# Layer 1's modulation units: sixteen for latent tokens alone, all 28 at other slabs

## Chip, cores and metric

The kernel runs on one core of a Trainium2 chip. The metric is the device time of one execution in microseconds (us), the median of several runs. The core's engines work side by side, each through its own list of instructions in order, and wait for each other by semaphores: TensorE (PE, matmuls; its weight loads are shown as PEld), VectorE (DVE), ScalarE (ACT), GpSimd (POOL) and SyncE (SP), which here issues all the transfers from memory.

## The reference, cut to what matters

A trunk of two layers. Each has a token mixer (gated linear attention in layer 0, windowed attention in layer 1) and a SwiGLU network (FFN). It works on 512 latent tokens (`x`) and 256 context tokens (`ctx`), with 1024 features. Shift, scale and gate of each sublayer come from two vectors, one for the latent tokens and one for the context tokens:

```
mod_x = einsum('bd,lde->lbe', silu(c), w_ada) + b_ada      # w_ada: 2 layers x 1024 x 6144
mod_c = einsum('d,lde->le', silu(c_ctx), w_ada) + b_ada
for i in range(DEPTH):                                     # DEPTH = 2
    last = i == DEPTH - 1
    sh1, sc1, g1, sh2, sc2, g2 = split(mod_x[i], 6)        # 1024 values each
    csh1, csc1, cg1, csh2, csc2, cg2 = split(mod_c[i], 6)
    hx = rmsnorm(x, norm_mix[i]) * (1 + sc1) + sh1
    hc = rmsnorm(ctx, norm_mix[i]) * (1 + csc1) + csh1
    ox, oc = mixer(hx, hc)                                 # context also feeds the latent tokens
    x = x + g1 * ox
    x = x + g2 * swiglu(rmsnorm(x, norm_ffn[i]) * (1 + sc2) + sh2)
    if not last:
        ctx = ctx + cg1 * oc
        ctx = ctx + cg2 * swiglu(rmsnorm(ctx, norm_ffn[i]) * (1 + csc2) + csh2)
return rmsnorm(x, norm_final)
```

In layer 1 the context tokens need only `csh1` and `csc1`: its gates and the FFN's modulation are used for latent tokens alone.

## The kernel before

Everything that is multiplied is split in two: a high part (rounded, made by ScalarE) and a low part (the rest, made by VectorE), and each product is three matmuls. Weights come in slabs of 256 columns, numbered `n` in the order of TensorE. For each slab SyncE loads the raw weights (`load_slab`), ScalarE makes the high part (`split`, or `form_high`), VectorE the low part (`split`, line 2005, or `form_low`, line 2562), and TensorE multiplies. Two sets of buffers alternate, so that `load_slab(n)` waits until slab n - 2 is done.

The stretch in question is the FFN of layer 0, slabs `F0` = 16 to `KV0` - 1 = 61. It has six parts. A part has input slabs (4, 4, 4, 3, 3, 4 of them: one row of 128 hidden units each, gate and up) and then four output slabs (`OUT0`), each for 256 of the 1024 output features and over the part's 4 or 3 rows. Part 0 begins at F0, part 1 at F0 + 8, part 2 at F0 + 16, part 3 at F0 + 24, part 4 at F0 + 31, part 5 at F0 + 38. From F0 + 3 on, input slabs are computed as seven products of half size (`SEVEN`), with sums of weight blocks (`form_sum`, line 2557) and of results (`part_sum` on ScalarE, line 1752; `gate_sum_one`, `up_sum_one` at lines 2577 and 2583, and so on, on VectorE). Seven-product slabs are 84 matmuls over 384 columns; output slabs of four rows are 48 over 512 or 256 columns.

The modulation vectors are made in units of 256 columns of `w_ada`. Units 12 to 15 are of layer 0, units 16 to 39 of layer 1. Unit a of layer 1 covers the columns (128 each) 16 + 2a and 17 + 2a of `mods`; from unit 24 on these are columns 64 to 95: gate of the mixer, and shift, scale and gate of the FFN. `UNIT_AT` says at which slab each of the units 12 to 39 is made. Before, that is: at the last input slab of part 0, the last two of parts 1 to 4 and the last three of part 5; at all four output slabs of parts 0 to 2, and at the first and third of parts 3 and 4.

A unit has these steps. SyncE loads it (1 MB, line 502) into the one buffer `ada_w`, right after the load of its slab in SyncE's queue, once the unit before it is accumulated (`ada_done`); the next slab's load is queued behind. VectorE adds up 8 blocks x 2 kinds of token, sixteen operations over 128x256 elements (`unit_acc`, lines 2106 and 2110), each of which waits for the one before the last. At the next slab TensorE sums over partitions by four small matmuls (`unit_sum`), after the first block of an output slab or the second product of a seven-product slab. Then VectorE closes the unit (`store_sum`, lines 2088, 2092, 2095) by three small operations.

The order on VectorE is written out by hand. In an output slab it is: `store_sum` of the slab before, `unit_acc`, `split(n + 1)`, `residual` (line 2121, once TensorE is done with the slab), so TensorE's next slab waits for the accumulations. In a seven-product slab with another behind it, `unit_acc` stands after `up_sum_one(n)` and ahead of the last four `form_low` of the next slab and of `times_gate` (line 2598), for which ScalarE's `high7(n)` waits; ScalarE's `part_sum(n + 1, 0)` is queued behind `high7(n)`, and TensorE's fourth product of slab n + 1 waits for it.

Of the kernel before, what the change touches and what calls it, by code (L numbers as in the profile page):

```python
# [30 lines left out]
AX = mybir.AxisListType  # L31

P = 128
D = 1024
DC = D // P
# [21 lines left out]
for part_, (f_, fc_) in enumerate(PARTS0):  # L57
    n_ = F0 + f_ + 4 * part_
    for j_ in range(fc_):
        IN0[n_ + j_] = f_ + j_  # L60
        if f_ + j_ >= 3:
            SEVEN[n_ + j_] = f_ + j_ - 3
        if part_ == 0 and j_ == 3 or 0 < part_ < 5 and j_ >= fc_ - 2 or part_ == 5 and j_ > 0:
            UNIT_AT[n_ + j_] = 12 + len(UNIT_AT)
    for e_ in range(4):
        OUT0[n_ + fc_ + e_] = (part_, e_, fc_)
        if part_ < 3 or part_ < 5 and e_ % 2 == 0:
            UNIT_AT[n_ + fc_ + e_] = 12 + len(UNIT_AT)
# [15 lines left out]
def trunk(nc, x, c, ctx_in, c_ctx, w_ada, b_ada, norm_mix, norm_ffn, gla_w_in, gla_w_gate_up, gla_b_gate_up,  # L84
# [240 lines left out]

        return n if n < R0 else n - R_SLOTS

    U1 = F0 - R_SLOTS

    def sum_no(a):  # L330

        return a if a < V0 else a - U1 + V0

    def u_set(a):

        return int(a >= U1)

# [337 lines left out]
    def _(pe):  # L675
# [439 lines left out]
        def ffn(l, n0, segs, per):  # L1115
            n, done = n0, l * FC
            for part, (f0, fc) in enumerate(PARTS):
                lead, after = int(part == 0), int(part == 2)
                if lead:

                    first_slab(n, 2 * l, segs, turn=U1 - 1 if l == 0 else None)
                    slab(n + 1, 0, h_in, segs, k_wait=h_wait(2 * l + 1, per), joint=True)
                m = n + 2 * lead
                with pe.Fori(0, fc // 2 - lead - after) as i:
                    for e in range(2):
                        slab(m + e, i, h_in, segs)
                if after:

                    for e in range(2):
                        m = n + fc - 2 + e  # L1130
                        slab(m, 0, h_in, segs)
                n += fc
                done += fc

                def ready(k, done=done, fc=fc):

                    if k in (0, fc - 1):
                        pe.wait_ge(a_ok, done - (k == 0))
                with pe.Fori(0, 2 - int(l == 1 and after)) as i:
                    for e in range(2):  # L1140
                        slab(n + e, i, a_in, segs, kc=fc, k_wait=ready)
                if l == 1 and after:
                    slab(n + 2, 0, a_in, segs, kc=fc)
                    slab(n + 3, 0, a_in, segs, kc=fc, by_chunk=True, between=early_result)
                n += 4
# [22 lines left out]
                              stop=(k == 3 and i == 2), skip=True)  # L1168
            last.then_inc(pd_ok if j < 6 else slab_done, 1)

        first_slab(F0, 0, BOTH, turn=U1 - 1)
        slab(F0 + 1, 0, h_in, BOTH, k_wait=h_wait(1, 2), joint=True)
        slab(F0 + 2, 0, h_in, BOTH)
        for n in range(F0 + 3, KV0):
            if n in SEVEN:
                for j in range(7):
                    product(n, j)
                    if j == 1 and n - 1 in UNIT_AT:
                        unit_sum(UNIT_AT[n - 1])
            else:  # L1180
                part, e, fc = OUT0[n]
                done = PARTS0[part][0] + fc

                def ready(k, done=done, fc=fc):

                    if k in (0, fc - 1):
                        pe.wait_ge(a_ok, done - (k == 0))
                slab(n, 0, a4_in, BOTH, kc=fc, k_wait=ready,
                     before={(0, 1): lambda: unit_sum(UNIT_AT[n - 1])} if n - 1 in UNIT_AT else {})


        first_slab(KV0, KV_EDGE, BOTH)
# [174 lines left out]
    def _(act):  # L1367
# [386 lines left out]
        def gate_one(n):  # L1754
            act.wait_ge(g_ok, SEVEN[n] + 1)
            silu(tmp[n % 2][:, 0:HT])
# [32 lines left out]
        form_high(F0 + 3, 2)  # L1789
        up0(F0 + 2, 2)  # L1790
        for n in range(F0 + 3, KV0):
            if n in SEVEN:
                after = n + 1 in SEVEN
                head = n - 1 not in SEVEN
# [14 lines left out]
                part_sum(n, 1)  # L1809
                if after:  # L1810
                    form_high(n + 1, 1)
                gate_one(n)
                if after:
                    form_high(n + 1, 2)
# [13 lines left out]
            else:  # L1828
                part, e, fc = OUT0[n]
                if e < 3:  # L1830
                    split(n + 1, 0, fc)
                elif part < 5:
                    for j in range(3):
                        form_high(n + 1, j)
                else:
                    split(n + 1)
                if part == 5:
                    for ch in range(2):
                        squares("ffn0", 2 * e + ch, 0)
                    for ch in range(2):  # L1840
                        raw_high("ffn0", KV_EDGE, 2 * e + ch, BOTH)
# [158 lines left out]
    def _(dve):  # L2000
# [82 lines left out]
        def store_sum(a, i=0):  # L2083

            dve.wait_ge(turned, a + 2 + i)
            dve.wait_ge(or_ok, u_set(a) + 1)
            part = u_acc[u_set(a)][:, 0, 0:P].rearrange("p (c n) -> p c n", n=32)
            dve.tensor_tensor(part, bank(7, 0, P).rearrange("p (c n) -> p c n", n=32),
                              every[u_set(a)][:, :].rearrange("p (o n) -> p o n", o=1).to_broadcast([P, 4, 32]), ALU.mult)\
               .then_inc(up_ok, 1)  # L2090
            dve.wait_ge(up_ok, 2 * sum_no(a) + 1 + i * 2)
            dve.tensor_reduce(den[:, :], part, AX.X, ALU.add).then_inc(up_ok, 1)
            dve.wait_ge(up_ok, 2 * sum_no(a) + 2 + i * 2)
            e = unit_cols(a) + i * 2
            dve.tensor_tensor(mods[:, bass.ds(e, 2), :], den[:, :].rearrange("p (m e) -> p e m", m=2),
                              v3(vec[:, bass.ds(V_BADA + e, 2)], 2), ALU.add).then_inc(mod_ok, 1)

        def unit_acc(a, i=0):

            dve.wait_ge(in_unit, 16 * (a + 1) + i * 16)  # L2100
            acc = u_acc[u_set(a)]
            for k in range(DC):
                for m in range(2):
                    j = 2 * k + m
                    if k == 0:
                        last = dve.tensor_scalar(acc[:, m, :], ada_w[:, 0, :], c_pre[:, 0, m:m + 1], None, ALU.mult)  # L2106
                    else:

                        dve.wait_ge(ua_ok, 15 * sum_no(a) + j - 1 + i * 15)
                        last = dve.scalar_tensor_tensor(acc[:, m, :], ada_w[:, k, :], c_pre[:, k, m:m + 1],  # L2110
                                                        acc[:, m, :], ALU.mult, ALU.add)
                    last.then_inc(ua_ok if j < 15 else ada_done, 1)
# [19 lines left out]

        dve.wait_ge(const_ok, N_CONST)
        dve.memset(c_pre[:, :, :], 0.0).then_inc(c_zero, 1)
        dve.memset(resets[:, :], 1.0).then_inc(resets_ok, 1)
        dve.wait_ge(resets_ok, 1)
        dve.memset(resets[:, 0:T:P], 0.0)
# [288 lines left out]
        for n in range(GO0, F0):  # L2426
            split(n + 1)
            plain(n, "gla", 2 * (n - GO0), 16, BOTH, False)
            raw_low(0, 2 * (n - GO0), BOTH)
            store_unit(unit_of(n))  # L2430
            if n == F0 - 1:
                dve.wait_ge(mod_ok, U1 + 1)
                shifts(0, 24)
            raw_low(0, 2 * (n - GO0) + 1, BOTH)

# [204 lines left out]
        form_sum(F0 + 3, 2)  # L2640
        form_low(F0 + 3, 1)
        form_low(F0 + 3, 2)
        up0(F0 + 2, 2)
        for n in range(F0 + 3, KV0):
            a_ = UNIT_AT.get(n)
            last_a = UNIT_AT.get(n - 1)
            if n in SEVEN:
                after = n + 1 in SEVEN
                if n - 1 not in SEVEN:
# [11 lines left out]
                    form_sum(n + 1, 0)  # L2661
                    form_low(n + 1, 0)
                gate_sum_one(n)
                if last_a is not None:
                    store_sum(last_a)
                if after:
                    form_sum(n + 1, 1)
                    form_sum(n + 1, 2)
                    form_low(n + 1, 1)
                    form_low(n + 1, 2)  # L2670
                    up_sum_one(n)
                    if a_ is not None:
                        unit_acc(a_)
                    form_low(n + 1, 3)
                    form_sum(n + 1, 3)
                    up_sum_two(n)
                    form_low(n + 1, 4)
                    form_low(n + 1, 5)
                else:
                    if a_ is not None:  # L2680
                        unit_acc(a_)
                    up_sum_one(n)
                    split(n + 1, 0, OUT0[n + 1][2])
                    up_sum_two(n)
                gate_sum_two(n)
                if after:
                    form_low(n + 1, 6)
# [1 line left out]
                low0(n)  # L2689
            else:  # L2690
                part, e, fc = OUT0[n]
                if last_a is not None:
                    store_sum(last_a)
                if part == 5 and e == 0:
                    scale_rows(48 + 8, V_NMIX + 8)
                if a_ is not None:
                    unit_acc(a_)
                if e < 3:
                    split(n + 1, 0, fc)
                elif part < 5:  # L2700
# [4 lines left out]
                    form_low(n + 1, 1)  # L2705
                else:
                    split(n + 1)
                if part < 5:
                    residual(n, 0, BOTH, 40, 2 * e, None)
                    if e == 3:  # L2710
# [228 lines left out]
```

## Time and profile before

| | us |
|---|---|
| median of 3 runs | 1681.86 (1681.06 to 1684.31) |
| the profiled execution, its own time | 1687.11 |
| its span, first to last instruction | 1685.4 |
| TensorE busy | 1584.0 |
| VectorE busy | 1083.0 |
| ScalarE busy | 665.2 |

The profile is of one execution. Its page gives the busy time of each engine, and the views cut it further: by stretch, by who waited for whom, or instruction by instruction. A busy TensorE may still be slow, since its clock is granted by the chip at full (1.0) or at half rate.

### The profile page before, as it was taken

To read this page: it belongs to the slowest core of one execution; us is meant where nothing else is said; L and a number is where in the kernel's file an instruction comes from. 1 tells how busy PE (TensorE), PEld (TensorE's weight loads), DVE (VectorE), ACT (ScalarE), POOL (GpSimd) and SP (SyncE) were. 2 spreads that over 40 slices of the span, in tenths; PEclk is the share of its full clock that TensorE was granted. 3 is DMA by queue.
4 is the path that set the end of the run, shared out by engine and by line. 5 is a ranking of instruction groups with operands and counts; after the bars stand their busy time and mean duration, and the time that the engine had idled before them with its cause. 6 is when DMAs were issued, how large, how long until landed. Compare 5 with 4: busy or idle time off the path is not lost.

```text
span 1685.4 us, 23337 instructions
## 1 busy us (share of the span) xinstructions
PE 1584.0 (94%) x9196; PEld 1363.8 (81%) x9196; DVE 1083.0 (64%) x1907; ACT 665.2 (39%) x1051; POOL 100.1 (6%) x95
## 2 busy tenths in 40 slices
PE   7999999999988989989898899999999999999998
PEld 4789988888886977978788788877778788888886
DVE  5655456444698888888878787788874633333334
ACT  5325367433641421423323234557763522222223
POOL 0000000000000000000000000006650000000002
PEclk8999999999999999989989899999999999999999
DMA  9333200033124324234233422431002332333322
GB/s 337 98 125 101 75 26 26 26 100 101 51 70 155 101 78 147 85 124 142 79 110 94 119 75 88 125 89 37 1 1 75 88 90 97 100 100 100 100 88 88
DMA packets 197842, 156.47 MB, mean 93 GB/s; under 512 B 7138, under 2 KB 194702, under 8 KB 197742
## 3 DMA queue, kind: packets, MB, share of 16 engines
q1 hardware_dynamic: 197742, 155.10, 30.2%
q8 instruction: 67, 1.10, 0.3%
q14 instruction: 33, 0.27, 0.1%
HBM read 149.84 MB, written 2.10 MB: 90 GB/s over the span
## 4 chain that ended last, share of the span: by engine, by line
PE 68%; DVE 18%; ACT 6%; DMA 4%; issue 3%; SPq 1%; DVEq 0%; ACTq 0%
PE ps L677 66%; DVE u_acc L2110 7%; DMA ada_w<-in_w_ada 2%; DVE w_lo L2005 1%; PE ps L1257 1%; DVE t_lo L2562 1%; DMA w_raw<-in_ffn_w_in 1%; ACT w_hi L1375 1%; ACT pr L1959 1%; DVE t_sum L2557 1%; DVE u_acc L2106 1%; DMA ada_pre<-in_w_ada 1%; DVE w_lo L2562 1%; DVE scaled L2061 1%; DVE tmp L2598 1%
## 5 line engine op out<-in xcount | busy, mean ns | idle before, releaser
L677 PE MATMUL ps<-h_hi,w_lo 128*128 128x512 f32 (+2 forms) x936 | 338.0, 361 | 0.0
L677 PE MATMUL ps<-h_hi,w_hi 128*128 128x512 f32 (+1 forms) x784 | 293.7, 375 | 4.2 <-DVE w_lo L2005 4.0
L677 PE MATMUL ps<-h_lo,w_hi 128*128 128x512 f32 (+1 forms) x784 | 286.4, 365 | 0.0
L2005 DVE TENSOR_TENSOR w_lo<-w_raw,w_hi 128x2048 fp32r<-128x2048 f32 (+1 forms) x57 | 128.5, 2254 | 198.4 <-ACT w_hi L1375 198.4
L677 PEld LDWEIGHTS ps<-h_hi,w_lo 128*128 128x128 f32 x936 | 177.4, 190 | 24.4
L677 PE MATMUL ps<-a_hi,w_lo 128*128 128x512 f32 (+1 forms) x528 | 192.4, 364 | 0.0
L1375 ACT ACTIVATE w_hi<-w_raw 128x2048 fp32r<-128x2048 f32 (+1 forms) x57 | 107.3, 1883 | 195.1 <-DMA w_raw<-in_ffn_w_in 98.3
L2110 DVE SCALAR_TENSOR_TENSOR u_acc<-ada_w,c_pre,u_acc 128x256 f32<-128x256 f32 x448 | 180.1, 479 | 0.0
L677 PEld LDWEIGHTS ps<-h_hi,w_hi 128*128 128x128 f32 x784 | 148.5, 189 | 34.5 <-issue 6.2
L677 PEld LDWEIGHTS ps<-h_lo,w_hi 128*128 128x128 f32 x784 | 148.7, 190 | 24.0
L677 PE MATMUL ps<-a_hi,out_hi_w 128*128 128x512 f32 (+1 forms) x352 | 128.6, 365 | 35.2 <-DVE w_lo L2005 33.7
L665 POOL TENSOR_SCALAR pr<-pr,rden 128x384 f32<-128x384 f32 x64 | 82.5, 1296 | 887.0 <-DVE rden L2845 886.7
L677 PE MATMUL ps<-a_lo,out_hi_w 128*128 128x512 f32 (+1 forms) x352 | 124.4, 353 | 0.0
L2121 DVE SCALAR_TENSOR_TENSOR xT<-ps,mods,xT 128x512 f32<-128x512 f32 (+2 forms) x142 | 82.5, 639 | 55.7 <-PE ps L677 55.7
L677 PEld LDWEIGHTS ps<-a_hi,w_lo 128*128 128x128 f32 x528 | 103.2, 195 | 15.6
L677 PEld LDWEIGHTS ps<-a_hi,out_hi_w 128*128 128x128 f32 x352 | 70.0, 199 | 51.1 <-DVE w_lo L2005 36.5
L677 PE MATMUL ps<-h_hi,form_hi 128*128 128x384 f32 x304 | 103.7, 341 | 5.0 <-DVE w_lo L2562 4.6
L677 PE MATMUL ps<-h_sums_lo,form_hi 128*128 128x384 f32 x304 | 106.7, 351 | 0.0
L677 PE MATMUL ps<-h_lo,form_hi 128*128 128x384 f32 x304 | 104.4, 343 | 0.0
L677 PEld LDWEIGHTS ps<-a_lo,out_hi_w 128*128 128x128 f32 x352 | 70.2, 200 | 7.1
L677 PE MATMUL ps<-h_sums_hi,form_hi 128*128 128x384 f32 x152 | 55.1, 363 | 21.3 <-ACT tmp L1752 21.3
L1732 ACT ACTIVATE form_hi<-t_sum 128x512 fp32r<-128x512 f32 x76 | 47.0, 627 | 70.3 <-DVE t_sum L2557 62.6
(320 smaller groups left out, 3125.1 us busy)
## 6 DMA issues: line engine op xcount, KB each, us to landing
w_raw<-in_ffn_w_in SPq DMA_DIRECT2D x88, 512.0 KB, 5.1
ada_w<-in_w_ada SPq DMA_DIRECT2D x41, 1024.0 KB, 5.3
w_raw<-in_gla_w_in SPq DMA_DIRECT2D x24, 512.0 KB, 4.9
w_raw<-in_ffn_w_out SPq DMA_DIRECT2D x40, 256.0 KB, 5.3
w_raw<-in_ffn_w_out SPq DMA_DIRECT2D x16, 512.0 KB, 4.4
ada_pre<-in_w_ada SPq DMA_DIRECT2D x7, 1024.0 KB, 11.5
w_raw<-in_gla_w_o SPq DMA_DIRECT2D x8, 512.0 KB, 6.8
w_raw<-in_swa_w_o SPq DMA_DIRECT2D x8, 512.0 KB, 4.6
```

The lines of the kernel that those rows point to most:

```text
L665: pool.tensor_scalar(pr[i % 4][:, 0:384], pr[i % 4][:, 0:384], rden[:, i % 4:i % 4 + 1], None, ALU.mult)\
L677: return pe.matmul(o, w, r, start=start, stop=stop, skip_group_check=skip)
L1257: last = pe.transpose(bank(4 + r, t * P, P), pr[i % 4][:, t * P:(t + 1) * P], ident[:, :])
L1375: act.activation(hi_of(n)[:, 0:kc, :], raw_of(n)[:, 0:kc, :], ACT.Copy).then_inc(whi_ok, 1)
L1732: act.activation(form_hi[j][:, :, :], form_from(n, j, w_raw, t_sum), ACT.Copy).then_inc(fh_ok, 1)
L1959: act.activation(pr[i % 4][:, 0:nk + 1], ps[:, sb:sb + nk + 1], ACT.Exp, bias=neg_max[:, i % 4:i % 4 + 1], scale=HD ** -0.5, accum_out=den ...
L2005: dve.tensor_tensor(w_lo[s][:, 0:kc, :], raw_of(n)[:, 0:kc, :], hi_of(n)[:, 0:kc, :].bitcast(F32), ALU.subtract).then_inc(wlo_ok, 1)
L2061: dve.scalar_tensor_tensor(scaled_t[ch % 2][:, s[0]:s[1]], xT[:, ch, s[0]:s[1]], amul[:, ch, c_:c_ + 1], rb[:, s[0]:s[1]], ALU.mult, ALU.m ...
L2106: last = dve.tensor_scalar(acc[:, m, :], ada_w[:, 0, :], c_pre[:, 0, m:m + 1], None, ALU.mult)
L2110: last = dve.scalar_tensor_tensor(acc[:, m, :], ada_w[:, k, :], c_pre[:, k, m:m + 1], acc[:, m, :], ALU.mult, ALU.add)
L2121: last = dve.scalar_tensor_tensor(xs, seg(slab_banks(n), ch, sg), mods[:, bass.ds(gate + d0 + ch, 1), int(sg == CTX)], xs, ALU.mult, ALU.add)
L2562: dve.tensor_tensor(form_from(n, j, w_lo, t_lo), form_from(n, j, w_raw, t_sum), form_hi[j][:, :, :].bitcast(F32), ALU.subtract).then_inc(f ...
```

## The change

1. `UNIT_AT` has other slabs: the last two input slabs of part 0, all four of part 1, the last two of parts 2 to 4, none of part 5. The output slabs stay as they are. Unit 12 is thus at slab F0 + 2, which isn't a seven-product slab, and its `unit_acc` stands by itself ahead of `up0(F0 + 2, 2)`. Before, units 12 to 39 were at 12 input slabs and 16 output slabs, and they are after.
2. Units from `LATENT` = 24 on are made for latent tokens alone: eight accumulations in place of sixteen, the even blocks in one half of `u_acc` and the odd in the other; the closing sum runs over both halves. The column sum on TensorE stays as it is. Columns 64 to 95 of `mods` for context tokens are set to zero once at the start.
3. TensorE, ScalarE and VectorE get branches for units below `U1` to be made on TensorE (`0 < now < U1`). With `U1` = 12 and units from 12 on, no slab takes them.

```
-        if part_ == 0 and j_ == 3 or 0 < part_ < 5 and j_ >= fc_ - 2 or part_ == 5 and j_ > 0:
+        if part_ == 0 and j_ >= 2 or part_ == 1 or 1 < part_ < 5 and j_ >= fc_ - 2:
             UNIT_AT[n_ + j_] = 12 + len(UNIT_AT)
...
-    U1 = F0 - R_SLOTS
+    U1 = 12
+    LATENT = 24
...
+    def acc_base(a):
+
+        whole = V0 + LATENT - U1
+        return 15 * min(sum_no(a), whole) + 7 * max(sum_no(a) - whole, 0)
...
@@ store_sum
+            if a >= LATENT:
+
+                both = u_acc[1][:, 0, 0:P].rearrange("p (m e n) -> p e m n", m=2, e=2)
+                dve.tensor_reduce(den[:, 0:2], both, AX.XY, ALU.add).then_inc(up_ok, 1)
+                dve.wait_ge(up_ok, 2 * sum_no(a) + 2)
+                dve.tensor_tensor(mods[:, e:e + 2, 0], den[:, 0:2], vec[:, V_BADA + e:V_BADA + e + 2], ALU.add)\
+                   .then_inc(mod_ok, 1)
+                return
...
@@ unit_acc
+            if a >= LATENT:
+
+                for k in range(DC):
+                    half = acc[:, k % 2, :]
+                    if k < 2:
+                        last = dve.tensor_scalar(half, ada_w[:, k, :], c_pre[:, k, 0:1], None, ALU.mult)
+                    else:
+
+                        dve.wait_ge(ua_ok, acc_base(a) + k - 1)
+                        last = dve.scalar_tensor_tensor(half, ada_w[:, k, :], c_pre[:, k, 0:1], half, ALU.mult, ALU.add)
+                    last.then_inc(ua_ok if k < DC - 1 else ada_done, 1)
+                return
...
         dve.memset(c_pre[:, :, :], 0.0).then_inc(c_zero, 1)
+        dve.memset(mods[:, 64:96, 1], 0.0)
...
         form_low(F0 + 3, 2)
+        unit_acc(12)
         up0(F0 + 2, 2)
```

## Rows read from the trace of the kernel before

**Rows 1.** The page: busy us (share of the span) xinstructions, by engine.
```profile
PE 1584.0 (94%) x9196; PEld 1363.8 (81%) x9196; DVE 1083.0 (64%) x1907; ACT 665.2 (39%) x1051; POOL 100.1 (6%) x95
```

**Rows 2.** TensorE's waits, 504 to 1030 us: us in total, times, longest.
```profile
PE ps L677 <- DVE w_lo L2005: 33.7, 13, 3.9
PE ps L677 <- ACT tmp L1752: 21.3, 6, 3.7
```

**Rows 3.** Stages: stretch, length, busy by engine, granted clock, DMA share, GB/s.
```profile
642.71:665.75 23.04, 19.91 (x112) 15.87 (x113) 20.44 (x50) 2.41 (x4) 0.00 (x0) 0.93 0.53 160
665.75:731.84 66.09, 62.56 (x352) 60.94 (x353) 55.67 (x106) 28.55 (x53) 0.00 (x0) 0.95 0.32 97
731.84:779.06 47.22, 40.68 (x225) 32.51 (x225) 40.88 (x97) 5.90 (x8) 0.00 (x0) 0.89 0.43 134
779.06:830.54 51.48, 47.95 (x269) 46.65 (x269) 44.54 (x89) 20.94 (x39) 0.00 (x0) 0.93 0.34 102
830.54:869.88 39.34, 31.79 (x170) 24.98 (x169) 28.85 (x64) 5.68 (x8) 0.00 (x0) 0.87 0.31 94
869.88:919.55 49.67, 46.15 (x262) 45.38 (x261) 42.41 (x83) 20.47 (x38) 0.00 (x0) 0.97 0.33 98
919.55:958.69 39.14, 31.58 (x169) 24.87 (x169) 28.84 (x64) 5.69 (x8) 0.00 (x0) 0.87 0.34 105
958.69:1029.06 70.37, 63.16 (x355) 61.63 (x353) 60.08 (x119) 28.53 (x52) 0.00 (x0) 0.95 0.33 98
```

**Rows 4.** VectorE's timeline, part 0's output: start us, us, instruction, [idle <-releaser].
```profile
508.99 0.28 DVE L2088 TENSOR_TENSOR u_acc<-ps,every 128x128 f32<-128x128 f32 x1
...
509.71 0.61 DVE L2106 TENSOR_SCALAR u_acc<-ada_w,c_pre 128x256 f32<-128x256 f32 x2
510.24 5.62 DVE L2110 SCALAR_TENSOR_TENSOR u_acc<-ada_w,c_pre,u_acc 128x256 f32<-128x256 f32 x14
...
521.18 0.62 DVE L2106 TENSOR_SCALAR u_acc<-ada_w,c_pre 128x256 f32<-128x256 f32 x2 [0.57 <-DMA ada_w<-in_w_ada]
```

**Rows 5.** SyncE's timeline in the same slab.
```profile
515.89 0.37 SPq L502 DMA_DIRECT2D ada_w<-in_w_ada  x1
```

**Rows 6.** VectorE's timeline, ends of two output slabs of part 5.
```profile
1046.52 2.19 DVE L2121 SCALAR_TENSOR_TENSOR xT<-ps,mods,xT 128x256 f32<-128x256 f32 x4 [0.81 <-PE ps L677]
...
1054.86 1.54 DVE L2121 SCALAR_TENSOR_TENSOR xT<-ps,mods,xT 128x256 f32<-128x256 f32 x3 [0.66 <-PE ps L677]
```

**Rows 7.** Instructions on the accumulator: ns min/median/max, first and last start.
```profile
L677 PE MATMUL ps<-u_acc,ones x256: 272/297/423, 77.2 to 1030.7; 128*32 128x128 f32 x128
```

**Rows 8.** VectorE's timeline, input slabs of parts 0 and 1.
```profile
488.36 1.01 DVE L2530 TENSOR_TENSOR tmp<-tmp,ps 128x256 f32<-128x256 f32 x2
...
565.14 0.55 DVE L2583 TENSOR_TENSOR tmp<-ps,tmp 128x384 f32<-128x384 f32 x1
...
573.11 0.96 DVE L2538 TENSOR_TENSOR a_lo<-tmp,a_hi 128x768 fp32r<-128x768 f32 x1 [0.91 <-ACT a_hi L1764]
...
587.67 0.96 DVE L2538 TENSOR_TENSOR a_lo<-tmp,a_hi 128x768 fp32r<-128x768 f32 x1 [0.91 <-ACT a_hi L1764]
...
594.73 0.61 DVE L2106 TENSOR_SCALAR u_acc<-ada_w,c_pre 128x256 f32<-128x256 f32 x2
```

**Rows 9.** TensorE's timeline: five instructions ahead of which it stood still.
```profile
608.21 0.69 PE L677 MATMUL ps<-h_sums_hi,form_hi 128*128 128x384 f32 x1 [3.52 <-ACT tmp L1752]
...
720.95 0.69 PE L677 MATMUL ps<-h_sums_hi,form_hi 128*128 128x384 f32 x1 [3.52 <-ACT tmp L1752]
...
842.42 0.80 PE L677 MATMUL ps<-a_hi,out_hi_w 128*128 128x512 f32 x1 [3.85 <-DVE w_lo L2005]
...
998.33 0.44 PE L677 MATMUL ps<-h_sums_hi,form_hi 128*128 128x384 f32 x1 [3.52 <-ACT tmp L1752]
...
1019.02 0.44 PE L677 MATMUL ps<-h_sums_hi,form_hi 128*128 128x384 f32 x1 [3.69 <-ACT tmp L1752]
```

**Rows 10.** VectorE's timeline at the start.
```profile
6.52 0.85 DVE L2141 COPY xT<-ps 128x256 f32<-128x256 f32 x2 [0.26 <-PE ps L820]
```

More of the change, by code:

```diff
@@ L1119, in ffn @@
                 if lead:
-                    first_slab(n, 2 * l, segs, turn=U1 - 1 if l == 0 else None)
+                    first_slab(n, 2 * l, segs)
                     slab(n + 1, 0, h_in, segs, k_wait=h_wait(2 * l + 1, per), joint=True)
@@ L1169, in product @@
             last.then_inc(pd_ok if j < 6 else slab_done, 1)
-        first_slab(F0, 0, BOTH, turn=U1 - 1)
+        first_slab(F0, 0, BOTH, turn=11)
         slab(F0 + 1, 0, h_in, BOTH, k_wait=h_wait(1, 2), joint=True)
@@ L1174, in _ @@
         for n in range(F0 + 3, KV0):
+            now, old = UNIT_AT.get(n, 0), UNIT_AT.get(n - 1, 0)
             if n in SEVEN:
@@ L1177, in _ @@
                     product(n, j)
-                    if j == 1 and n - 1 in UNIT_AT:
-                        unit_sum(UNIT_AT[n - 1])
+                    if j == 1 and old >= U1:
+                        unit_sum(old)
+                    if j == 1 and 0 < now < U1:
+                        unit(now)
+                    if j == 4 and 0 < now < U1:
+                        unit_turn(now)
             else:
@@ L1187, in ready @@
                         pe.wait_ge(a_ok, done - (k == 0))
-                slab(n, 0, a4_in, BOTH, kc=fc, k_wait=ready,
-                     before={(0, 1): lambda: unit_sum(UNIT_AT[n - 1])} if n - 1 in UNIT_AT else {})
+                at_ = {}
+                if old >= U1:
+                    at_[0, 1] = lambda: unit_sum(old)
+                if 0 < now < U1:
+                    at_[0, 2] = lambda: unit(now)
+                    at_[1, fc - 1] = lambda: unit_turn(now)
+                slab(n, 0, a4_in, BOTH, kc=fc, k_wait=ready, before=at_)
         first_slab(KV0, KV_EDGE, BOTH)
@@ L1791, in _ @@
         for n in range(F0 + 3, KV0):
+            now = UNIT_AT.get(n, 0)
             if n in SEVEN:
@@ L1811, in _ @@
                     form_high(n + 1, 1)
+                if 0 < now < U1:
+                    unit_row(now)
                 gate_one(n)
@@ L1836, in _ @@
                     split(n + 1)
+                if 0 < now < U1:
+                    unit_row(now)
                 if part == 5:
@@ L2087, in store_sum @@
             part = u_acc[u_set(a)][:, 0, 0:P].rearrange("p (c n) -> p c n", n=32)
+            e = unit_cols(a) + i * 2
             dve.tensor_tensor(part, bank(7, 0, P).rearrange("p (c n) -> p c n", n=32),
@@ L2091, in store_sum @@
             dve.wait_ge(up_ok, 2 * sum_no(a) + 1 + i * 2)
+            if a >= LATENT:
[5 more added lines that the diff above has]
+                return
             dve.tensor_reduce(den[:, :], part, AX.X, ALU.add).then_inc(up_ok, 1)
             dve.wait_ge(up_ok, 2 * sum_no(a) + 2 + i * 2)
-            e = unit_cols(a) + i * 2
             dve.tensor_tensor(mods[:, bass.ds(e, 2), :], den[:, :].rearrange("p (m e) -> p e m", m=2),
@@ L2107, in unit_acc @@
                     else:
-                        dve.wait_ge(ua_ok, 15 * sum_no(a) + j - 1 + i * 15)
+                        dve.wait_ge(ua_ok, acc_base(a) + j - 1)
                         last = dve.scalar_tensor_tensor(acc[:, m, :], ada_w[:, k, :], c_pre[:, k, m:m + 1],
@@ L2431, in _ @@
             if n == F0 - 1:
-                dve.wait_ge(mod_ok, U1 + 1)
+                dve.wait_ge(mod_ok, 13)
                 shifts(0, 24)
@@ L2642, in _ @@
         form_low(F0 + 3, 2)
+        unit_acc(12)
         up0(F0 + 2, 2)
         for n in range(F0 + 3, KV0):
-            a_ = UNIT_AT.get(n)
-            last_a = UNIT_AT.get(n - 1)
+            now, old = UNIT_AT.get(n, 0), UNIT_AT.get(n - 1, 0)
             if n in SEVEN:
@@ L2663, in _ @@
                 gate_sum_one(n)
-                if last_a is not None:
-                    store_sum(last_a)
+                if old >= U1:
+                    store_sum(old)
                 if after:
@@ L2671, in _ @@
                     up_sum_one(n)
-                    if a_ is not None:
-                        unit_acc(a_)
+                    if now >= U1:
+                        unit_acc(now)
                     form_low(n + 1, 3)
@@ L2679, in _ @@
                 else:
-                    if a_ is not None:
-                        unit_acc(a_)
+                    if now >= U1:
+                        unit_acc(now)
                     up_sum_one(n)
@@ L2684, in _ @@
                     up_sum_two(n)
+                if 0 < now < U1:
+                    store_unit(now)
                 gate_sum_two(n)
@@ L2691, in _ @@
                 part, e, fc = OUT0[n]
-                if last_a is not None:
-                    store_sum(last_a)
+                if old >= U1:
+                    store_sum(old)
                 if part == 5 and e == 0:
                     scale_rows(48 + 8, V_NMIX + 8)
-                if a_ is not None:
-                    unit_acc(a_)
+                if now >= U1:
+                    unit_acc(now)
                 if e < 3:
@@ L2707, in _ @@
                     split(n + 1)
+                if 0 < now < U1:
+                    store_unit(now)
                 if part < 5:
```

## The prediction, made before the change was run

> **What bounds the kernel now.** I read the busy line of the page first: TensorE is busy for 94% of the span and VectorE for 64% [rows 1]. So time can be had only where TensorE stands still or runs slowly. The view of waits, for TensorE alone and for the stretch in which all 28 moved units lie, names two releasers: 33.7 us in 13 waits for VectorE's low halves of output slabs (line 2005), and 21.3 us in 6 waits for ScalarE's copies in seven-product slabs (line 1752) [rows 2]. The windows by stage then show a second loss. The granted clock is at its lower level (1.2 of 2.4 GHz) for part of every stage, and length x (1 - clock) is what that costs: 1.6, 3.3, 5.2, 3.6, 5.1, 1.5, 5.1 and 3.5 us in the eight stages from 642.71 us on, 28.9 us together [rows 3].
>
> What a unit costs VectorE is in the timeline of one output slab [rows 4]. The closing chain runs from 508.99 to 509.71 us (0.7 us); the sixteen accumulations run from 509.71 to 515.86 us, about 6.1 us until the next operation can start. The fourteen long ones take 5.62 us, which is one of 0.48 us and thirteen steps of 0.396 us. SyncE issues the next unit's transfer at 515.89 us [rows 5], and its accumulations start at 521.18 us, released by that transfer [rows 4]: 5.3 us. One turn of this loop is 5.3 + 6.1 = 11.4 us. TensorE needs less: two output slabs without units in the last part end 8.34 us apart [rows 6]. The eight records of a column sum last 0.30 us each but overlap [rows 7]; I take 0.5 us for them, so 8.9 us for a slab with a unit. **The output slabs are bound by the loop of transfer and accumulation, not by TensorE.**
>
> In seven-product slabs, an undisturbed one lasts 587.67 - 573.11 = 14.56 us [rows 8]. A unit delays VectorE's last products of the slab, ScalarE queues behind them, and TensorE stops at the fourth product of the next slab: 3.52 us each in parts 1 and 2 and twice, 3.52 and 3.69, in part 5 [rows 9].
>
> **The change, stage by stage.** Times are of the profiled execution.
>
> A latent unit (24 to 39) has eight accumulations. Each waits for the one before the last, as now, so I keep the step [rows 4]: 8 x 0.396 = 3.17 us less, 2.9 us left. The closing chain keeps its three operations; I count nothing for the smaller ones (between 0 and 0.2 us each).
>
> Unit 12 moves ahead of `up0(F0 + 2, 2)`, which starts at 488.36 us [rows 8]. VectorE has work without a pause from there to the output slab, so all of it comes 6.1 us later, the fourth product of slab F0 + 3 with it, and its column sum makes TensorE wait until 494.5 us. ScalarE's copies for that slab queue behind `up0`. Unit 13 then takes the place that unit 12 had, with one closing chain more: **+6.9 us** for the first output slab. From below it is 0.7 us, if a pause hid the accumulations, from above 8.5 us if low clock is added. The transfers have room: unit 12's is issued a slab earlier, unit 13's at 494.5 us for a use at 503 us. The four output slabs of part 0 have a full unit each now and after: 0. SyncE's queue there holds each slab's load behind the same kind of unit load as now.
>
> Part 1 gets full units in all four of its seven-product slabs, where two had one. The first would start after line 2583 at 565.14 + 0.47 = 565.61 us; now one starts at 594.73 in slab F0 + 10 and the stop ends at 608.21 us [rows 8, 9], 13.48 us later. So the fourth product of slab F0 + 9 comes at 579.1 us. For slabs with full units one after the other the trace has a sample: the two stops of part 5 end 20.69 us apart [rows 9], because the chain of VectorE and the slab load queued behind the unit's load take that long. Two such periods give 620.5 us against 608.21: **+12.3 us**. At best it is the three stops, two more than now, with no clock loss, +7; at worst each period is 2 us longer, +16.
>
> Part 1's output slabs 2 and 3 have units 24 and 25, latent. Loop: 5.3 + 2.9 = 8.2 us, below TensorE's 8.9, so TensorE becomes the bound: 23.04 us [rows 3] becomes 17.9, **-5.1**.
>
> Part 2, seven products: the stop shrinks from 3.52 to 0.35 us, and the low clock of its stage goes. Of the 3.3 us some lies within the stop itself: the four products from 720.95 to 731.84 us take 10.89 us [rows 3, 9] where 4/7 of 14.56, or 8.32, is undisturbed, so 2.6 us. 3.17 + 2.6: **-5.7**. Part 2, output: 47.22 us becomes 4 x 8.9 + 0.1, **-11.5**. Part 3, seven products: 3.17 and four fifths of 3.6: **-6.0**; part 4, 3.17 and four fifths of 1.5: **-4.5**.
>
> Output slabs of parts 3 and 4 (three rows, three quarters of 8.34 = 6.26 us): the first goes from 842.42 - 830.54 = 11.88 [rows 3, 9] to 8.7 us, still VectorE-bound; then 6.8, 6.3 and 6.8 us, and 0.6 us at the next slab, whose weights now land only just in time: 29.2 us against 39.34 and 39.14 [rows 3]: **-10.1 and -9.9**.
>
> Part 5 loses its three units. 4 x 14.56 + 0.4 = 58.6 us against 70.37 [rows 3], **-11.8**, and **-0.5** for the column sum in its first output slab.
>
> The memset of 32 values lies on VectorE before line 2141, which waits for TensorE (0.26 us) [rows 10]: 0, at most 0.1 us. The kernel ends with no other difference: layer 1 waits for all units at its load of Q, and the last one is now done earlier.
>
> Sum: +6.9 + 12.3 - 5.1 - 5.7 - 11.5 - 6.0 - 4.5 - 10.1 - 9.9 - 11.8 - 0.5 = **-45.9 us**. The profiled execution took 1687.11 us (span 1685.4); the median of the runs is 1681.86, 0.3% less, which leaves the difference as it is: **1636 us**.
>
> One rule prices the accumulations otherwise. The Trainium skill (VectorE: DVE Perf Modes, "The TRN2 errata") gives such an operation 58 cycles beside one for each element, at 0.96 GHz; worked out from that page as an estimate, 0.33 us for 256 elements, or 2.6 us saved in a unit and a total some 3 us longer. The trace has the duration (0.396 us), so that is used.
>
> **Rivals.**
> *The clock stays low.* The stops shrink, but the clock falls as before. For it: no stage from part 1 on is free of it, and small stops remain. Against: it goes with the stops; the stages with most of them for their length are at 0.87, the one with a single stop in 49.67 us is at 0.97 [rows 3]. It would cost the 28.9 us of the stages: -17, 1665 us. The rule that speaks for it is in the Trainium skill (TensorE: Matmul & The Clock Gate, "HAM oscillation"): a wait that comes back in each step makes the clock drop anew in each.
> *The transfer becomes the bound.* A loop of landing plus 2.9 us stays hidden only while a unit lands within 6.0 us. If contention with the slab's load, which is now issued at another moment, made it half as long again as the 5.3 us, some 7.8 us, nine output slabs are 1.8 us longer each: +16, 1652 us. Against: the unit's load is still issued ahead of the slab's, as at 515.89 us.
> *Slower: eight accumulations take as long as sixteen.* If an accumulation had to wait for the result of its predecessor, the step would be some 0.76 us (6.1/8). Then nothing is gained in parts 1 to 4, and +6.9 + 12.3 - 12.3 leaves +6.9 us: 1689 us. The gains of parts 1 to 4, 52.8 us, hang on the 3.17 us, so the sign turns where a latent unit is shorter by less than 0.4 us. Against it: the two running sums alternate as the two token kinds do now.
>
> **How the numbers follow.** Forecast 78%, with a range of its own of 1628 to 1648 from the bounds of +6.9 and +12.3 and of the unit's landing; low clock 7%, transfer 11%, slower 4%. The range of 1628 to 1655 takes in the transfer case and leaves out the clock case, the slower one and the forecast's tails. A difference below 0.2% (3.4 us) can't be told from none: faster 95%, same 1%, slower 4%.
>
> **What would show it.** Latent units of 2.9 us; output slabs of part 2 9 us apart with no wait for line 2005; stops of under 1 us in parts 2 to 4, three of about 3.6 us in part 1, none in part 5; clock 1.0 in nearly all stages after part 1; the first output slab of part 0 some 7 us later, of part 1 some 19 us later. A loop that still takes over 10 us in part 2, or a low clock there with stops gone, would prove me wrong.

## The result: 1639.4 us, 2.5% faster

The changed kernel takes 1639.41 us (median of 4 runs, 1638.66 to 1641.18), the kernel before beside it 1682.28 us. The ratio is 0.9746, with a 95% interval of 0.9729 to 0.9762: 42.9 us less, where 45.9 were forecast. The two profiled spans are 1685.4 and 1639.5 us, 45.9 us apart; the forecast was worked out from the first, so the stages are compared in them. That they differ by 3 us more than the medians comes from which executions were profiled: 1687.11 us is 4.8 above the median before, 1641.18 us is 1.8 above the median after.

TensorE's waits in the changed kernel, 504 to 1019 us, line 2026 being the old 2005, 1768 the old 1752 (us in total, times, longest). They answer to [rows 2]:

```profile
PE ps L683 <- DVE w_lo L2026: 17.9, 10, 3.1
PE ps L683 <- ACT tmp L1768: 12.5, 6, 4.4
PE ps L683 <- DVE w_lo L2604: 1.9, 5, 0.8
PE ps L683 <- DVE a_lo L2580: 1.5, 2, 0.7
```

Both waits have about halved, 33.7 to 17.9 and 21.3 to 12.5 us. Of the kernel before, part 0's output and part 1's input (stretch, length, busy by engine, granted clock, DMA share, GB/s) were:

```profile
504.77:551.77 47.00, 38.29 (x224) 30.91 (x225) 41.28 (x98) 5.90 (x8) 0.00 (x0) 0.96 0.48 150
551.77:619.13 67.36, 63.83 (x352) 62.62 (x353) 55.94 (x106) 28.80 (x53) 0.00 (x0) 0.92 0.30 91
```

The stages of the changed kernel's trace answer to [rows 3] from the third row on; the first two are part 1's input and its first two output slabs, and the last is part 5's output:

```profile
557.39:635.03 77.64, 66.22 (x368) 63.47 (x369) 68.89 (x144) 28.83 (x53) 0.00 (x0) 0.93 0.36 105
635.03:658.62 23.59, 18.31 (x113) 14.92 (x113) 20.52 (x48) 3.50 (x4) 0.00 (x0) 1.00 0.39 125
658.62:678.07 19.45, 19.45 (x112) 15.85 (x113) 15.09 (x35) 2.85 (x4) 0.00 (x0) 0.91 0.60 189
678.07:738.12 60.05, 59.69 (x354) 58.48 (x353) 48.60 (x89) 28.44 (x52) 0.00 (x0) 1.00 0.37 111
738.12:774.00 35.88, 35.88 (x226) 29.90 (x226) 29.71 (x67) 6.34 (x8) 0.00 (x0) 1.00 0.53 168
774.00:819.49 45.49, 45.13 (x271) 43.92 (x269) 37.24 (x71) 20.64 (x38) 0.00 (x0) 1.00 0.39 120
819.49:848.77 29.28, 27.60 (x169) 22.39 (x169) 21.00 (x46) 5.32 (x8) 0.00 (x0) 1.00 0.39 121
848.77:894.40 45.63, 45.09 (x261) 43.84 (x262) 37.72 (x70) 20.82 (x39) 0.00 (x0) 1.00 0.39 120
894.40:924.70 30.30, 27.84 (x170) 22.40 (x169) 20.92 (x46) 5.33 (x8) 0.00 (x0) 1.00 0.39 116
924.70:983.65 58.95, 58.74 (x337) 58.24 (x337) 42.76 (x68) 28.76 (x53) 0.00 (x0) 1.00 0.23 63
983.65:1019.00 35.35, 33.91 (x194) 29.54 (x194) 26.93 (x39) 17.41 (x24) 0.00 (x0) 1.00 0.29 91
```

Read the first number after each stretch against the old one, and the clock, third from the end. In part 2's output TensorE is busy for all of its 35.88 us, and from part 2 on no stage is below a clock of 1.00. The terms side by side (the first two are later positions in the span, taken from the start of slab F0 + 2 at 468.77 and 467.72 us):

| | forecast | measured |
|---|---|---|
| first output slab of part 0 later | +6.9 | +6.8 |
| part 1, input slabs | +12.3 | +10.3 |
| part 1, output slabs 2 and 3 | -5.1 | -3.6 |
| part 2, input / output | -5.7 / -11.5 | -6.0 / -11.3 |
| part 3, input / output | -6.0 / -10.1 | -6.0 / -10.1 |
| part 4, input / output | -4.5 / -9.9 | -4.0 / -8.8 |
| part 5, input / output | -11.8 / -0.5 | -11.4 / -0.2 |

They sum to -44.3 us. Another 1.05 us had been won before slab F0 + 2, where nothing of the change works but the memset; part 0's output gave 0.1 us and what comes behind the FFN 0.3 us; the rest is rounding.

What VectorE does in part 2's output slabs (start us, us, instruction, [idle <-releaser]) answers to [rows 4]:

```profile
742.94 0.61 DVE L2136 TENSOR_SCALAR u_acc<-ada_w,c_pre 128x256 f32<-128x256 f32 x2
743.46 2.46 DVE L2140 SCALAR_TENSOR_TENSOR u_acc<-ada_w,c_pre,u_acc 128x256 f32<-128x256 f32 x6
745.84 1.22 DVE L2026 TENSOR_TENSOR w_lo<-w_raw,out_hi_w 128x1024 fp32r<-128x1024 f32 x1
...
751.16 0.62 DVE L2136 TENSOR_SCALAR u_acc<-ada_w,c_pre 128x256 f32<-128x256 f32 x2 [1.01 <-DMA ada_w<-in_w_ada]
751.69 2.46 DVE L2140 SCALAR_TENSOR_TENSOR u_acc<-ada_w,c_pre,u_acc 128x256 f32<-128x256 f32 x6
...
756.35 2.19 DVE L2162 SCALAR_TENSOR_TENSOR xT<-ps,mods,xT 128x256 f32<-128x256 f32 x4 [1.05 <-PE ps L683]
...
765.27 2.19 DVE L2162 SCALAR_TENSOR_TENSOR xT<-ps,mods,xT 128x256 f32<-128x256 f32 x4 [1.19 <-PE ps L683]
```

A latent unit lasts from 742.94 to 745.84 us, 2.9 us, and two accumulations begin 8.2 us apart (742.94, 751.16): 2.9 us of work, and 5.3 us until the next unit has landed. The results of two slabs come 8.92 us apart (756.35, 765.27), and now it is VectorE that waits for TensorE.

TensorE's stops, by the instruction behind each, answer to [rows 9]:

```profile
493.60 0.43 PE L683 MATMUL ps<-u_acc,ones 128*32 128x128 f32 x8 [3.18 <-DVE u_acc L2151]
...
583.99 0.48 PE L683 MATMUL ps<-h_sums_hi,form_hi 128*128 128x384 f32 x1 [4.36 <-ACT tmp L1768]
...
604.53 0.53 PE L683 MATMUL ps<-h_sums_hi,form_hi 128*128 128x384 f32 x1 [3.54 <-ACT tmp L1768]
...
625.04 0.55 PE L683 MATMUL ps<-h_sums_hi,form_hi 128*128 128x384 f32 x1 [3.52 <-ACT tmp L1768]
...
729.69 0.45 PE L683 MATMUL ps<-h_sums_hi,form_hi 128*128 128x384 f32 x1 [0.36 <-ACT tmp L1768]
```

The first is unit 12's column sum waiting for its accumulations; the next three are the stops of part 1's full units, 20.5 us apart; the last is a latent unit's stop.

### The profile page after: what moved, and what is told of

Same layout as the page of the kernel before. It is cut to its first block, busy times and chain, and to the rows that moved or that the text cites. A ratio compares the mean times of both kernels' runs of the same rounds, so it can differ in the third digit from the quotient of the medians.

```text
span 1639.5 us, 23210 instructions
## 1 busy us (share of the span) xinstructions
PE 1563.2 (95%) x9196; PEld 1346.9 (82%) x9196; DVE 1033.5 (63%) x1780; ACT 665.8 (41%) x1051; POOL 100.1 (6%) x95
## 4 chain that ended last, share of the span: by engine, by line
PE 71%; DVE 15%; ACT 6%; DMA 4%; issue 3%; SPq 1%; DVEq 0%; ACTq 0%
PE ps L683 69%; DVE u_acc L2151 4%; DMA w_raw<-in_ffn_w_in 1%; DVE t_lo L2604 1%; DVE w_lo L2026 1%; PE ps L1273 1%; DVE t_sum L2599 1%; DMA ada_w<-in_w_ada 1%; ACT pr L1980 1%; ACT w_hi L1391 1%; DVE w_lo L2604 1%; DMA ada_pre<-in_w_ada 1%; DVE scaled L2082 1%; DVE u_acc L2140 1%; PE ps L1278 1%
## 5 line engine op out<-in xcount | busy, mean ns | idle before, releaser
L683 PE MATMUL ps<-a_hi,w_lo 128*128 128x512 f32 (+1 forms) x528 | 188.5, 357 | 0.0
L683 PE MATMUL ps<-a_hi,out_hi_w 128*128 128x512 f32 (+1 forms) x352 | 123.6, 351 | 18.0 <-DVE w_lo L2026 16.5
L683 PE MATMUL ps<-a_lo,out_hi_w 128*128 128x512 f32 (+1 forms) x352 | 120.1, 341 | 0.0
L2151 DVE SCALAR_TENSOR_TENSOR u_acc<-ada_w,c_pre,u_acc 128x256 f32<-128x256 f32 x224 | 90.0, 480 | 0.0
L683 PE MATMUL ps<-a_hi,w_hi 128*128 128x512 f32 x176 | 68.7, 391 | 0.0
L683 PE MATMUL ps<-a_lo,w_hi 128*128 128x512 f32 x176 | 68.5, 389 | 0.0
## 6 DMA issues: line engine op xcount, KB each, us to landing
ada_pre<-in_w_ada SPq DMA_DIRECT2D x7, 1024.0 KB, 11.4
```

The lines of the kernel that those rows point to most:

```text
L683: return pe.matmul(o, w, r, start=start, stop=stop, skip_group_check=skip)
```

## Experiments

Each run stands beside measurements of the kernel before of its own round, whose medians lie between 1682.28 and 1684.24 us. Where a run is compared with the changed kernel, a difference of under some 2 us in the medians therefore says little, and the stages say more.

**Moving alone and halving alone.**

```
# moving alone, against the changed kernel: no unit is latent
-    LATENT = 24
+    LATENT = 40
# halving alone, against the changed kernel
-        if part_ == 0 and j_ >= 2 or part_ == 1 or 1 < part_ < 5 and j_ >= fc_ - 2:
+        if part_ == 0 and j_ == 3 or 0 < part_ < 5 and j_ >= fc_ - 2 or part_ == 5 and j_ > 0:
...
-        unit_acc(12)
         up0(F0 + 2, 2)
```

> The changed kernel with LATENT = 40: the units are at the new slabs, but all 28 have sixteen accumulations. My theory (gain and loss are separate terms, read stage by stage): moving alone loses. 6.7 us at slab F0 + 2/3, 10.3 us in part 1's seven-product slabs, against 11.6 us won in part 5; parts 2 to 4 as in the kernel before, each stop 3.5 us. Sum +5.4: 1687.7 us, in all 1684 to 1691. Rival A (the move itself is what brought the gain, since part 5 is freed and the units no longer stand ahead of the end): under 1670 us. Rival B (halving is worth the same everywhere and the move is neutral): 1682 us.

> Halving alone: UNIT_AT of the kernel before, unit_acc(12) by itself taken out again, LATENT = 24 kept. Units 24 to 39 then stand from the last input slab of part 2 to part 5. My theory: no loss at part 0 and part 1; part 2's output -11.3, part 3 -16, part 4 -13, part 5 -10 us (stops of 0.35 us for 3.5, clock back): -50 us, 1632 us, 7 us faster than the changed kernel. Rival A (part 5 has to be free of units): over 1640 us. Rival B (the gain needs both, as the latent units are too few behind part 2's middle): 1650 us or more.

Moving alone is slower: 1689.8 us against 1684.24 beside it, ratio 1.0030 (1.0019 to 1.0042), 5.6 us. Three of its stages, part 1's input, part 2's output and part 5's input:

```profile
557.89:636.04 78.15, 67.81 (x369) 65.06 (x369) 68.91 (x144) 29.06 (x53) 0.00 (x0) 0.91 0.36 104
...
748.02:795.18 47.16, 39.47 (x225) 31.62 (x225) 40.87 (x97) 5.90 (x8) 0.00 (x0) 0.93 0.46 141
...
975.10:1033.35 58.25, 58.25 (x338) 58.25 (x337) 41.30 (x65) 28.50 (x52) 0.00 (x0) 1.00 0.23 64
```

Part 2's output is at 47.16 us, as before the change (47.22), so what it won comes from the halving. Part 5's is 12.1 us shorter and part 1's 10.8 us longer. Both rivals of that expectation are out.

Halving alone takes 1637.26 us, ratio 0.9720 (0.9703 to 0.9736). It is ahead of the changed kernel by 2 us in the medians and 3.7 us in the spans, not by the 7 I expected. Its stages of part 2's input and part 5's input:

```profile
662.11:730.21 68.10, 64.41 (x353) 62.65 (x354) 52.74 (x98) 28.81 (x53) 0.00 (x0) 0.92 0.32 98
...
916.89:979.86 62.97, 60.94 (x352) 58.34 (x353) 52.28 (x98) 28.60 (x53) 0.00 (x0) 1.00 0.38 109
```

Part 5 with three latent units is 4 to 5 us longer than without any (58.95 or 58.25), where stops of 0.35 us and column sums of some 0.5 us would make 1 to 2. And part 2's input, with a full unit still at its third slab, is 2 us longer than before (66.09) at a clock of 0.92 for 0.95.

**Full units off the seven-product slabs that have another behind them.**

```
-        if part_ == 0 and j_ >= 2 or part_ == 1 or 1 < part_ < 5 and j_ >= fc_ - 2:
+        if part_ in (0, 1, 2) and j_ == 3 or part_ == 3 or part_ == 4 and j_ > 0 or part_ == 5:
```

(`unit_acc(12)` by itself is out here too.)

> Halving, with the full units taken off the seven-product slabs that have another behind them: one unit at the last input slab of parts 0, 1 and 2, latent ones at all of part 3's, the last two of part 4's and all of part 5's; output slabs as before. The theory gives: part 1's input -6, part 2's input -6, its output -7 (its first slab has a full unit), part 3 -16, part 4 -13, part 5 -9.5: -57.5 us, 1625 us. Rival A (a latent unit in the first slab of a part, where VectorE also makes that slab's own low halves, stops TensorE by some 3 us): 1632 us. Rival B (the stops of full units there are not what costs; the transfers are): no better than halving alone, 1632 us or more.

1635.48 us, ratio 0.9709 (0.9693 to 0.9725): -48.8 us, short of the -57.5 expected. The waits of TensorE in its part 5, four latent units:

```profile
PE ps L683 <- ACT tmp L1768: 3.4, 5, 1.2
PE ps L683 <- DVE w_lo L2604: 0.7, 2, 0.5
```

Its stages of part 1's, part 2's and part 5's input:

```profile
550.76:610.92 60.16, 59.58 (x345) 58.29 (x345) 48.60 (x87) 28.55 (x53) 0.00 (x0) 1.00 0.28 81
...
657.56:718.22 60.66, 60.66 (x345) 59.90 (x345) 48.87 (x87) 29.04 (x53) 0.00 (x0) 0.97 0.26 77
...
912.10:978.03 65.93, 62.34 (x361) 58.44 (x361) 55.66 (x109) 28.44 (x53) 0.00 (x0) 1.00 0.37 108
```

Parts 1 and 2 won about what was expected in their input (7.2 and 5.4 us, 6 each expected). Part 5's input won 4.4 us where 9.5 were expected, and part 3 13.2 us where 16 were: 0.35 us is the stop of a latent unit behind a slab without one; behind another latent unit it is 1.2 us. The stops are not all of it. Two stops in a row of part 5 end 17.41 us apart (952.18 and 969.59 us), against 14.56 for a slab without a unit: 2.85 us, of which the stop is 1.2 and the column sum some 0.5; the rest lies in TensorE's busy time and isn't explained by a row here.

**The same places, latent units accumulated later.** `late(n)` is true for a latent unit in a seven-product slab with another behind it. Its load goes out behind the next slab's load, and its accumulations stand behind `gate_sum_two`:

```
@@ SyncE
-            if n in UNIT_AT:
+            if n - 1 in UNIT_AT and late(n - 1):
+                load_unit(UNIT_AT[n - 1])
+            if n in UNIT_AT and not late(n):
                 load_unit(UNIT_AT[n])
@@ VectorE
-                    if now >= U1:
+                    if now >= U1 and not late(n):
                         unit_acc(now)
                     form_low(n + 1, 3)
...
                 gate_sum_two(n)
+                if late(n):
+                    unit_acc(now)
```

> The third experiment's places of units, but in a seven-product slab with another behind it a latent unit is accumulated later, after gate_sum_two, where VectorE waits 1.1 us for ScalarE anyway, and its load is queued behind the next slab's load in place of ahead of it. If the stops there come from VectorE's last products standing behind the accumulations: stops of part 3 and 5 (0.35 to 1.2 us) go, -6 us against the third experiment. If they come from VectorE's total work for the slab, the later start of the next slab's operations gives it back: no difference.

1624.95 us, ratio 0.9656 (0.9640 to 0.9672): -57.9 us, the fastest here, 14.5 us ahead of the changed kernel and 10.5 us ahead of the third experiment. The waits of TensorE in its part 5, and that stage:

```profile
PE ps L689 <- DVE w_lo L2610: 0.5, 2, 0.3
```

```profile
906.07:966.77 60.70, 60.52 (x360) 58.69 (x361) 54.99 (x109) 28.69 (x53) 0.00 (x0) 1.00 0.43 131
```

No stop for ScalarE's copy is left there: 65.93 became 60.70 us, and part 3's input went from 48.35 to 45.44. With part 4 that is 8.2 us in the stages that this edit touches, 6 were expected; some 2.7 us more lie in parts 1 and 2, which it doesn't touch (part 2's input, for one, was at a clock of 1.00 for 0.97). VectorE's total work is the same, so that was not what stopped TensorE.

Which of the two moves did it is open, since they were tried only together, and the second has rows of its own. Loads of input weights issued from 912 to 962 us, first in the third experiment, then here (KB each, median us from issue to landing), and between them a wait of VectorE in the third experiment's part 5 that is gone here:

```profile
w_raw<-in_ffn_w_in SPq DMA_DIRECT2D x6, 512.0 KB, 6.7
DVE t_sum L2599 <- DMA w_raw<-in_ffn_w_in: 1.8, 2, 0.9
w_raw<-in_ffn_w_in SPq DMA_DIRECT2D x4, 512.0 KB, 4.6
```

In the third experiment a slab's load is queued behind a unit's, which waits for the unit before it; the two loads go out at 927.57 and again at 944.89 us, 17.3 us apart, as far as the slabs themselves. So the accumulations ahead of the last products and the slab load behind the unit's load are both possible causes of the longer slabs.

**Chained accumulations.** The changed kernel with one running sum in a latent unit (the closing sum, not shown here, runs over that one alone):

```
-                    half = acc[:, k % 2, :]
-                    if k < 2:
+                    half = acc[:, 0, :]
+                    if k < 1:
...
-                        dve.wait_ge(ua_ok, acc_base(a) + k - 1)
+                        dve.wait_ge(ua_ok, acc_base(a) + k)
```

> The changed kernel, but a latent unit has one running sum: each of its eight accumulations waits for the one just before it, and the closing sum takes that one alone. It asks what the step would be if the operations were chained, the rival that would have made the change slower. If the step stays at 0.396 us (one operation's result is there when the next starts): 1639 us. If it is the operation's own 0.48 us and little more: a unit of 3.9 us, stops in parts 2 to 4 of 1.3 us, loop 9.2 us: 1645 us. If it is 0.76 us: a unit of 6 us as before, 1686 us.

1648.44 us, ratio 0.9784 (0.9768 to 0.9800). One unit of it:

```profile
755.05 0.35 DVE L2136 TENSOR_SCALAR u_acc<-ada_w,c_pre 128x256 f32<-128x256 f32 x1 [1.42 <-DMA ada_w<-in_w_ada]
755.45 3.61 DVE L2140 SCALAR_TENSOR_TENSOR u_acc<-ada_w,c_pre,u_acc 128x256 f32<-128x256 f32 x7
758.97 1.22 DVE L2026 TENSOR_TENSOR w_lo<-w_raw,out_hi_w 128x1024 fp32r<-128x1024 f32 x1
```

The unit takes 3.9 us. The step is (3.61 - 0.48)/6 = 0.52 us, against 0.396 with two sums in turn: a chain costs a third more, not twice. One more microsecond in each of 16 units made 9.0 us in the medians and 8.4 us in the spans. The 0.76 us that I had put on the slower rival's step does not occur here, and even chained the change would have been some 2% faster.

**Half transfers.** In the kernel before and in the changed one, units 12 to 39 load four of their eight blocks. These kernels leave out the other half of each unit's weights (the accumulations read what the buffer held), and all operations stay:

```
+            m = 4 if a >= 12 else DC
-            sp.dma_start(ada_w[:, :, :], w_ada[l][:, bass.ds((e + i) * 256, 256)]...
+            sp.dma_start(ada_w[:, 0:m, :], w_ada[l][0:m * P, bass.ds((e + i) * 256, 256)]...
```

> The kernel before, but units 12 to 39 load only four of their eight blocks of w_ada (the other four are summed from what the buffer held), so a unit's transfer is 0.5 MB for 1 MB; all sixteen accumulations stay. It asks whether the transfer is in the loop of the output slabs. My theory, that the loop is transfer plus accumulation (5.3 + 6.1 us): the transfer falls to some 3.5 us, then VectorE's own order (residual, closing chain, accumulations, split: 10.2 us) is the bound; some nine output slabs get 1.2 us shorter, 11 us, 1673 us. The rival, that VectorE alone bounds these slabs: no change, 1683 us.

> The changed kernel with the same half transfers for units 12 to 39. Latent units' slabs are bound by TensorE by my theory, so only the four output slabs with full units behind a full unit gain (1.2 us each), and part 4's output 0.7 to 1.5 us, where a slab's load landed late beside a unit's: -6 us against the changed kernel. If the latent slabs still hang on the transfer: -15 us or more.

The kernel before becomes 1671.87 us, ratio 0.9938 (0.9919 to 0.9957): -11.0 us. VectorE in its part 0, the start of two units:

```profile
520.37 0.61 DVE L2108 TENSOR_SCALAR u_acc<-ada_w,c_pre 128x256 f32<-128x256 f32 x2
...
530.51 0.61 DVE L2108 TENSOR_SCALAR u_acc<-ada_w,c_pre 128x256 f32<-128x256 f32 x2
```

A turn is 10.14 us (520.37 to 530.51) where it was 11.47 (509.71 to 521.18 [rows 4]), and the wait for `ada_w` that stood at 521.18 [rows 4] is gone. So the transfer is in the loop. The gain is the 11 us that were expected.

The changed kernel becomes 1635.40 us (ratio 0.9715, 0.9696 to 0.9733), 4.0 us less by the medians and 5.6 by the spans. Its stages of part 0's, 2's and 4's output:

```profile
511.56:554.44 42.88, 38.20 (x224) 30.92 (x225) 41.01 (x98) 5.89 (x8) 0.00 (x0) 0.96 0.36 110
...
732.70:768.58 35.88, 35.88 (x226) 29.90 (x226) 29.46 (x67) 6.35 (x8) 0.00 (x0) 1.00 0.39 118
...
888.93:918.17 29.24, 27.61 (x169) 22.39 (x169) 20.98 (x46) 5.32 (x8) 0.00 (x0) 1.00 0.32 95
```

Part 2's output, latent units alone, is 35.88 us with either size: there the transfer costs nothing. The gain is in part 0's full units (4.0 us), in part 1's output, where the first two slabs have full units (41.26 us for 43.04, 1.8 us), and in part 4 (1.1 us); about 1 us of it is lost again ahead of part 0's output, which starts at 511.56 us for 510.51.

**Unit 12 back in its place.**

```
-        if part_ == 0 and j_ >= 2 or part_ == 1 or 1 < part_ < 5 and j_ >= fc_ - 2:
+        if part_ == 0 and j_ == 3 or part_ == 1 or 1 < part_ < 5 and j_ >= fc_ - 2 or part_ == 5 and j_ == 3:
...
-        unit_acc(12)
         up0(F0 + 2, 2)
```

> The changed kernel with its first term taken back: unit 12 at slab F0 + 3 again, the others one place earlier, the last one at part 5's last input slab. The term of +6.8 us goes; part 1's third output slab has a full unit again (+2.3), part 5's last input slab a latent one (+0.9): -3.6 us against the changed kernel. Rival (the delay of the first output slab is made up later in part 0, where the loop rather than the start counts): no difference or slower.

1636.67 us, ratio 0.9726 (0.9710 to 0.9743), 2.7 us below the changed kernel (span 4.8 us below), where 3.6 were expected. The first output slab starts at 503.39 us for 510.51, and parts 0 and 1:

```profile
503.39:550.21 46.82, 39.72 (x225) 31.77 (x225) 41.20 (x98) 5.91 (x8) 0.00 (x0) 0.93 0.47 146
550.21:627.78 77.57, 66.21 (x368) 63.45 (x369) 68.91 (x144) 28.81 (x53) 0.00 (x0) 0.93 0.36 105
627.78:673.37 45.59, 38.18 (x225) 30.83 (x225) 37.92 (x89) 5.96 (x8) 0.00 (x0) 0.96 0.47 146
```

The later start is not made up in part 0 (46.82 and 46.88 us), so it counted in full; 2.6 us come back as one more full unit in part 1's output.

## Why the prediction was right, and where it was off

The sum held because in most stages the thing that bound them could be read from a row. Point by point:

- *Output slabs bound by transfer plus accumulation.* Shown by the half transfers in the kernel before, and by the latent loop of 8.2 us under slabs of 8.9, where half transfers change nothing.
- *The step stays at 0.396 us.* Six long operations take 2.46 us, one of them 0.48: (2.46 - 0.48)/5 = 0.396.
- *Unit 12 delays all of VectorE by a unit.* `up0` starts at 493.37 us, 6.07 us behind the start of the accumulations (487.30); +6.8 us in all, shown to count by taking it back.
- *Part 1.* The mechanism held, three stops and a period of 20.5 us for 20.69; the term was 2 us too large. The first stop was 4.36 us long, not 3.52, and yet ended 0.7 us earlier in the stage than forecast (26.6 us behind its start for 27.3), which no row here explains; the two periods were 0.3 us shorter together. The four products behind the last stop take 9.99 us (625.04 to 635.03, clock 0.83), where behind the old one they took 10.92 (608.21 to 619.13, clock 0.75): the term had kept the old stretch of low clock as it was. For part 1's last two output slabs it is the other way round: the clock of that stage is 0.91, and 19.45 us came where 17.9 were forecast.
- *Part 4's input* was 0.5 us short (by its own terms, 3.17 and four fifths of 1.5, the forecast is 4.4, not 4.5).
- *Part 4's output*, 1.1 us short. ScalarE waited for a slab's load that had gone out 0.9 us ahead of a unit's (902.47 and 903.33 us):

```profile
ACT out_hi_w L1391 <- DMA w_raw<-in_ffn_w_out: 10.4, 1, 10.4
```

  TensorE stood still for 0.65 us after it. With half transfers the stage takes 29.24 us. So transfers did get in each other's way, at one place and not at nine; but what came late there was the slab's load, where the transfer rival had the unit's.
- *The clock goes with the stops*, with the short ones at least. Every stage from part 2 on is at 1.00, with stops of up to 0.75 us and one of 1.4 us at the end of part 5's output. The rival by which it stays low (1665 us) is out. Of the rule of the Trainium skill that stood beside it (TensorE: Matmul & The Clock Gate, "HAM oscillation") the prediction left out a condition: the page's case has waits for transfers of several microseconds. Waits of under 1.5 us that come back, with no drop, don't contradict it; they are another case. And a long stop doesn't always bring the clock down: part 1's first two output slabs have one of 3.08 us between them and are at 1.00.
- *The slower rival* had a true mechanism, and a price worked out from nothing better than half the work in the old time; measured, the step is 0.52 us, not 0.76.

The profiled spans differ by just the forecast, and that is partly luck. Part 1's input cost 2.0 us less than forecast, but its output and part 4's won 1.5 and 1.1 us less and the other terms together 1.0 us less; the 1.6 us missing were made up in places that no term counts, 1.05 us of them ahead of slab F0 + 2. By the medians the gain was 42.9 us, 3 us under the forecast.

## What to carry to other kernels

When an engine waits at the same place in every turn, find the loop behind it (here one buffer: land, use up, issue again) and add up its parts: anything taken from a part counts until the next bound, and no further. Work that moves must be priced at its new place by a row in which such work already stands so; the same unit of 6.1 us costs 2.8 us more than a latent one in an output slab (47.22 and 35.88 us for four), and between 5 and 7 us in a seven-product slab with another behind it (10.3 us for two in part 1; 7.2 us won there when one was taken out). What stands ahead of an operation that a neighbour waits for can cost more than its own length, by the low clock behind the stop or by the load that goes out later. Moving latent accumulations behind that operation, and their load behind the next slab's, brought 8 us in the stages concerned with the same instructions.

## What the runs showed of the hardware

- Accumulations over 128x256 elements follow each other every 0.396 us with two sums in turn and every 0.52 us when each needs the one just before.
- Half the bytes did not halve a transfer. A unit's loads in the kernel before and in the one with half transfers, 500 to 1030 us (KB each, median us from issue to landing):

```profile
ada_w<-in_w_ada SPq DMA_DIRECT2D x27, 1024.0 KB, 5.3
ada_w<-in_w_ada SPq DMA_DIRECT2D x27, 512.0 KB, 3.6
```

- The order in the queue counts. In the changed kernel the unit loads that went out right behind a slab's load landed after 7.8 to 8.4 us (those at 694.45, 776.02, 849.58 and 903.33 us), all others between 493 and 891 us after 5.1 to 5.7 us. The slab loads pay when they go out second: 6.7 us in the third experiment, 4.6 us in the one with the late accumulations.
- The clock and the length of stops: in the ten traces, from 500 to 1020 us, not one of the 151 stops of TensorE that the profiles list with up to 1.74 us was followed by a granted clock below 1.00 in the next 5 us. Of the 98 stops of 2.18 to 4.38 us, 82 were. In the changed kernel the stage at 658.62 us began behind a stop of 2.2 us and was at 0.91, but the 5 us behind the one of 3.08 us at 647.19 us were at 1.00. What makes the difference among the long ones is not shown.
